# Hybrid decoder layer with a 32-expert MoE: 32 KB rows for the gate-up weights, four 4 MB places, and the add-back moved into the next gate-up

## The reference

```
out = h + merged @ w_out                       # h: (272, 1024), then only the 256 real tokens
u   = rms_norm(out)
top4 of softmax(u @ w_router)                  # 32 experts
gu  = u_rows @ w_gate_up[e] + b_gate_up[e]     # (rows, 1024) @ (1024, 2048)
gate, up = split(gu);  gate = min(gate, 7);  up = clip(up, -7, 7)
act = (up + 1) * gate * sigmoid(1.702 * gate)
y  += weight * (act @ w_down[e] + b_down[e])   # (rows, 1024) @ (1024, 1024)
```

## Time and profile before

| | us |
|---|---|
| median of 3 runs | 1257.53 |
| the runs | 1256.41 to 1257.77 |
| profiled execution, its own time | 1257.31 |
| its span (first to last instruction) | 1255.5 |
| TensorE busy in the span | 1178.8 |
| mean granted TensorE clock | 0.983 |

### The profile page before, as it was taken

The page is one execution under the profiler, slowest core; times in us unless marked ns, Lnnn a source line. Parts: engine busy times, 40 slices in busy tenths (PEclk is TensorE's granted clock), DMA queues, the critical chain, the costliest instruction groups (busy, mean ns, idle before and its releaser), DMA issues.

```text
span 1255.5 us, 14149 instructions
## 1 busy us (share of the span) xinstructions
PE 1178.8 (94%) x5825; PEld 657.1 (52%) x5825; DVE 302.8 (24%) x551; ACT 133.1 (11%) x270; POOL 4.7 (0%) x12
## 2 busy tenths in 40 slices
PE   9999999999999999999898989898898989898998
PEld 7877788888743435534352534343443434353533
DVE  2155222312302322304030303122121303030322
ACT  2233311101200000101000000001010100000000
POOL 0000001000000000000000000000000000000000
PEclk9999998999999999999999999999999999999999
DMA  9722332336799999999999999999999999999996
GB/s 380 324 98 100 110 105 97 134 116 264 278 392 423 428 428 426 430 426 426 431 428 426 429 430 428 428 429 430 426 429 430 428 428 430 429 428 429 429 420 271
DMA packets 38002, 446.37 MB, mean 356 GB/s; under 512 B 4016, under 2 KB 5168, under 8 KB 6352
## 3 DMA queue, kind: packets, MB, share of 16 engines
q1 hardware_dynamic: 37344, 443.63, 84.6%
q10 hardware_dynamic: 624, 2.25, 0.5%
HBM read 444.81 MB, written 1.05 MB: 355 GB/s over the span
## 4 chain that ended last, share of the span: by engine, by line
PE 68%; DMA 28%; issue 2%; DVE 2%; SPq 0%; ACT 0%; DVEq 0%; ACTq 0%
DMA ring<-in_w_down 23%; PE ps L511 20%; PE ps L807 18%; PE ps L830 11%; PE ps L770 5%; DMA arena<-in_w_down 4%; PE ps L796 3%; PE ps L869 3%; PE ps L851 1%; PE ps L816 1%; DVE arena L1424 1%; PE ps L825 0%; PE ps L570 0%; PE ps L643 0%; SPq L438 0%
## 5 line engine op out<-in xcount | busy, mean ns | idle before, releaser
L807 PE MATMUL ps<-ring,arena 128*64 128x512 f32 x1392 | 419.6, 614 | 36.9 <-DMA ring<-in_w_gate_up 30.5
L807 PEld LDWEIGHTS ps<-ring,arena 128*64 128x64 f32 x1392 | 137.6, 141 | 301.4 <-issue 301.4
L511 PE MATMUL ps<-arena,ring 128*128 128x256 f32 (+1 forms) x1184 | 268.2, 383 | 1.1 <-DVE arena L1305 1.1
L511 PEld LDWEIGHTS ps<-arena,ring 128*128 128x128 f32 x1184 | 221.5, 190 | 38.4 <-issue 6.6
L830 PE MATMUL ps<-ring,arena 128*64 128x512 f32 x672 | 200.9, 599 | 26.8 <-DMA arena<-in_w_down 18.0
L807 PE MATMUL ps<-arena 128*64 128x512 f32 x464 | 207.1, 599 | 0.0
L830 PEld LDWEIGHTS ps<-ring,arena 128*64 128x64 f32 x672 | 65.3, 138 | 146.3 <-issue 146.3
L1404 DVE COPY arena<-ps 128x1024 f32<-128x1024 f32 x16 | 19.6, 1224 | 420.2 <-PE ps L807 417.3
L830 PE MATMUL ps<-arena 128*64 128x512 f32 x224 | 102.0, 610 | 0.0
L1130 ACT ACTIVATE arena<-ps 128x1024 f32<-128x1024 f32 x16 | 16.4, 1023 | 583.5 <-PE ps L807 553.5
L1397 DVE TENSOR_TENSOR arena<-ps,arena 128x512 f32<-128x512 f32 x64 | 41.1, 684 | 145.8 <-PE ps L816 145.8
(11 more groups left out here) (208 smaller groups left out, 574.5 us busy)
## 6 DMA issues: line engine op xcount, KB each, us to landing
ring<-in_w_gate_up SPq DMA_DIRECT2D x95, 2048.0 KB, 26.9
ring<-in_w_down SPq DMA_DIRECT2D x47, 2048.0 KB, 24.1
arena<-in_w_gate_up SPq DMA_DIRECT2D x32, 2048.0 KB, 31.2
ring<-in_mix_w SPq DMA_DIRECT2D x37, 1024.0 KB, 5.5
arena<-in_w_down SPq DMA_DIRECT2D x16, 2048.0 KB, 26.1
ring<-in_w_down SPq DMA_DIRECT2D x2, 1024.0 KB, 30.6
arena<-in_consts ACTq DMA_DIRECT2D x1, 1424.0 KB, 12.0
arena<-in_xT SPq DMA_DIRECT2D x2, 544.0 KB, 4.3
```

The lines of the kernel that those rows point to most:

```text
L511: last = mm(ps[:, PROJ + half, 0:rhs.shape[-1]], w[:, k, half * P:(half + 1) * P], rhs, start=(k == 0), stop=(k == KC - 1))
L807: last = mm(ps[half, bank + b], columns[:, j, half], w[x][:, at:at + 512], start=(j == 0), stop=(j == 7))
```

## The change

1. **Rows and places.** From lap 3 on (`pair(2)`), gate-up weights are loaded in units of 4 MB: half of one expert, 128 rows of 32 KB, four weight rows each. There are four places of 4 MB (`quad`): three are the ring, one (`last_quad`) lies in the arena, where the order of regions and constants is changed to make it contiguous. Down units stay at 2 MB with rows of 16 KB and use halves of those places. The rows of laps 0 to 2 keep their lengths, but take other weight rows, since which weight row meets which partition now follows (h p j) with four neighbours; the copy that orders the token columns (`u2tok`) changes with it.
2. **Release.** TensorE multiplies gate-up in two halves (`gate_up_quad`), each of which waits for two 4 MB units and reports both of them used at its end. The four down units of a lap wait for the first half of the gate-up ahead of them (`gu_used`), the next gate-up for the second half and for the two halves of down (`dn_used`).
3. **Add-back.** `add_back(m - 1)` now stands between the halves of gate-up in `pair(m)`, for m from 1 on; so the bias is added in pair 1, with the add-back of lap 0. In the last pair the add-back of lap 14 still stands behind its down weights, as `add_back_by_halves`.
4. **Transition.** The expert loads start one projection unit earlier; the first unit of lap 1 is issued with unit 7 of lap 0, behind the reads of `wr`; units 6 and 7 of lap 1 wait for `gu_used` 5 and 6, where they waited for 6 and 8. The transposes of the token weights (L942 before) move from ahead of the first gate-up into it.
5. **Retention.** `rv_meta` and `rs_meta` have 128 rows, of which GpSimd sets all to zero ahead and 16 are filled, so that L634's matmuls take 128 rows. The decay constants come in a DMA of their own.

```diff
-    for name, n in (("ones", P), ("ident", P), ("heads2", P), ("halves", 2), ("eps", 1), ("eps64", 1), ("slopes", 2 * HEADS), ("fold", EXPERTS),
-                    ("tri", P), ("from_1", TOK), ("alibi", SCW), ("decay", RH * TOK), ("decay_meta", RH * TOK)):
+    for name, n in (("decay", RH * TOK), ("decay_meta", RH * TOK), ("ones", P), ("ident", P), ("heads2", P), ("halves", 2), ("eps", 1), ("eps64", 1), ("slopes", 2 * HEADS), ("fold", EXPERTS),
+                    ("tri", P), ("from_1", TOK), ("alibi", SCW)):
...
-N_CONST_EARLY = CONST_COLS["tri"][0]
+EARLY, LATE = CONST_COLS["ones"][0], CONST_COLS["tri"][0]
...
-        rv_tok, rv_meta = cut(r_rv, 0, (2, D)), cut(r_rv, 2 * D, (D,), META)
+        rv_tok, rv_meta = cut(r_rv, 0, (2, D)), cut(r_rv, 2 * D, (D,))
...
-        rs, rs_meta = cut(r_p, 0, (RH, 3 * BLK)), cut(r_p, RH * 3 * BLK, (RH, TOK), META)
+        rs, rs_meta = cut(r_p, 0, (RH, 3 * BLK)), cut(r_p, RH * 3 * BLK, (RH, TOK))
...
+        last_quad = arena[:, end_p - 2048:end_p + 6144]
+        spare = (last_quad[:, 0:4096], arena[:, end_rg - 4096:end_rg], last_quad[:, 4096:8192])
...
-        COUNT, WT, LOGIT, BIAS = 2, 3, 3, 1
+        COUNT, WT, LOGIT, BIAS = 2, 6, 3, 1
...
+        def slot_of(unit):
+            return (unit + SLOTS - 1) % SLOTS
+        homes = tuple((double(d), pair_landed[d]) for d in range(DOUBLES)) + ((spare[0], spare_landed[0]), (spare[2], spare_landed[2]))
+        def quad(m, n):
+            odd = m if isinstance(m, int) else 0
+            q = ((1 if odd % 2 else 3) + n) % 4
+            return last_quad if q == 3 else ring[:, 4 * q:4 * q + 4].rearrange("p a b -> p (a b)"), quad_landed[q]
+        def half_quad(odd, n):
+            return quad(odd, n // 2)[0][:, 4096 * (n % 2):4096 * (n % 2 + 1)]
...
-            if j == 4:
+            if j == 7:
                 return spare[1], spare_landed[1], 16
-            dst, arrived = homes[{0: 0, 1: 1, 2: 2, 3: 3, 5: 4, 7: 5}[j]]
+            dst, arrived = homes[j]
             return dst, arrived, 16
 
-        def place(m, q, odd=None):
-
-            if isinstance(m, int):
-                turn_no = 12 * m + q + 6
-                dst, arrived = homes[turn_no % 8]
-                return dst, arrived, 16 * (turn_no // 8 + 1)
-            turn_no = 12 * odd + q + 6
+        def place(m, q):
+            turn_no = 12 * m + q + 6
             dst, arrived = homes[turn_no % 8]
-            return dst, arrived, 24 * (m - odd) + 16 * (turn_no // 8 + 1)
+            return dst, arrived, 16 * (turn_no // 8 + 1)
...
+            nc.gpsimd.memset(rv_meta, 0.0).then_inc(zeros_set, 1)
+            pool.wait_ge(att_done, PAIRS)
+            nc.gpsimd.memset(rs_meta, 0.0).then_inc(zeros_set, 1)
...
-                return w_gate_up[bass.ds(2 * lap + x, 1), :, :].rearrange("o (i p j) n -> (o p) i (j n)", i=4, j=2)[:, i]
+                return w_gate_up[bass.ds(2 * lap + x, 1), :, :].rearrange("o (h p i j) n -> (o p) h i (j n)", h=2, i=2, j=2)[:, i // 2, i % 2]
...
-                i, jj = divmod(j, 2)
-                return w_gate_up[2 * lap:2 * lap + 2].rearrange("o (i p j) n -> p i j o n", i=4, j=2)[:, i, jj]
+                h, jj = divmod(j, 4)
+                return w_gate_up[2 * lap:2 * lap + 2].rearrange("o (h p j) n -> p h j o n", h=2, j=4)[:, h, jj]
+            def four_rows_source(lap, n):
+                h, x = divmod(n, 2)
+                return w_gate_up[bass.ds(2 * lap + x, 1), :, :].rearrange("o (h p j) n -> (o p) h (j n)", h=2, j=4)[:, h]
...
-                for j in (0, 1, 2, 3, 4, 5, 7):
-                    if j < 3:
-                        sp.wait_ge(proj_done, 2 * (27 + 2 * j + 1))
-                    elif j < 5:
+                for j in (0, 1, 2, 3, 7, 4, 5):
+                    if j == 7:
                         sp.wait_ge(proj_read, AT[("wr", KC - 1)] + 1)
+                        dst, arrived, _ = place(0, 0)
+                        sp.dma_start(dst.rearrange("p (o n) -> p o n", o=2), both_experts_source(1, 0)).then_inc(arrived, 16)
                     else:
-                        sp.wait_ge(proj_done, 2 * (33 + (j - 5) + 1))
+                        sp.wait_ge(proj_done, 2 * (26 + 2 * j + 1))
...
+                for q in range(1, 12):
+                    if q == 1:
 
                         sp.wait_ge(logit_folded, 1)
                         src = both_experts_source(0, 6)
                         for x, (lo, hi) in ((0, (0, 2048)), (1, (0, 1024)), (1, (1024, 2048))):
                             sp.dma_start(split_place(x, lo, hi), src[:, x, lo:hi]).then_inc(split_landed, 16)
                         sp.wait_ge(u2_turned, 2)
-                    elif q < 6:
+                    elif q < 8:
                         sp.wait_ge(gu_used, q - 1)
-                    elif q < 8:
-                        sp.wait_ge(gu_used, 2 * q - 6)
...
+            def gate_up_quads(m, odd, lap):
                 for n in range(4):
-                    dst, arrived, _ = place(m, first_q + n, odd)
-                    slot_free(m, first_q + n)
-                    src = down_both_source(lap, n // 2, n % 2)
-                    dst = dst.rearrange("p (o n) -> p o n", o=2)
-                    if n == 3 and pieces == 2:
+                    if n < 2:
+                        sp.wait_ge(gu_used, 8 * m + 6 + 2 * n)
+                    else:
+                        sp.wait_ge(dn_used, 4 * m - 6 + 2 * n)
+                    dst, arrived = quad(odd, n)
+                    sp.dma_start(dst, four_rows_source(lap, n)).then_inc(arrived, 16)
+            def down_halves(m, odd, lap):
+                for n in range(4):
+                    sp.wait_ge(gu_used, 8 * m + 10 + 2 * (n // 2))
+                    sp.dma_start(half_quad(odd, 8 + n), down_source(lap, n)).then_inc(down_landed[n], 16)
+            def last_down_units(m):
+                for n in range(4):
+                    sp.wait_ge(gu_used, 8 * m + 10 + 2 * (n // 2))
+                    dst = half_quad(0, 8 + n).rearrange("p (o n) -> p o n", o=2)
+                    sp.dma_start(dst, down_both_source(14, n // 2, n % 2)).then_inc(down_landed[n], 16)
+                for n in range(4):
+                    sp.wait_ge(gu_used, 8 * m + 14 + 2 * (n // 2))
+                    dst = half_quad(1, n).rearrange("p (o n) -> p o n", o=2)
+                    src = down_both_source(15, n // 2, n % 2)
+                    if n < 3:
+                        sp.dma_start(dst, src).then_inc(tail_landed[n], 16)
+                    else:
                         for jj in range(2):
                             part = slice(jj * D, (jj + 1) * D)
-                            sp.dma_start(dst[:, :, part], src[:, :, part]).then_inc(tail_landed[jj], 16)
-                    else:
-                        sp.dma_start(dst, src).then_inc(arrived, 16)
+                            sp.dma_start(dst[:, :, part], src[:, :, part]).then_inc(tail_landed[3 + jj], 16)
...
+                gate_up_quads(m, 0, lap_1)
+                down_halves(m, 0, lap_0)
+                gate_up_quads(m + 1, 1, lap_2)
+                down_halves(m + 1, 1, lap_1)
+            gate_up_quads(last_m, 0, 15)
+            last_down_units(last_m)
...
+            def gate_up_quad(m, odd, h):
+                w = []
+                for x in range(2):
+                    dst, arrived = quad(odd, 2 * h + x)
+                    pe.wait_ge(arrived, 16 * m - 16)
+                    w.append(dst)
+                for jj in range(4):
+                    j = 4 * h + jj
+                    for b in range(4):
+                        at = jj * 2048 + b * 512
+                        for x, half in enumerate(halves):
+                            last = mm(ps[half, GATE + b], xeT[:, j, half], w[x][:, at:at + 512], start=(j == 0), stop=(j == 7))
+                            if jj == 3 and b == 3:
+                                last.then_inc(gu_used, 2)
...
+            def add_back_by_halves(m):
+                for b in range(4):
+                    pe.wait_ge(eout_ready, 2 * m + 1 + b // 2)
+                    pe.wait_ge(added, 4 * m - 1 + b)
+                    for c in range(2):
+                        at = (2 * b + c) * P
+                        last = mm(add_ps[:, b % 2, c], e_out[:, at:at + P], selwT, start=True, stop=True)
+                    last.then_inc(summed, 1)
...
+                pe.wait_ge(wgt_ready, 1)
+                for t in range(2):
+                    last = turn(ps[0:EXPERTS, WT, t * P:(t + 1) * P], wgt[:, t], ident)
+                last.then_inc(wgt_turned, 1)
...
-                        gate_up(i, lambda q: place(m, q, odd), xeT)
+                    for h in range(2):
+                        if h == 1:
+                            pe.wait_ge(selwT_ready, m)
+                            pe.wait_ge(eout_ready, 2 * m)
+                            add_back(m - 1, isinstance(m, int) and m == 1)
+                        if odd is None:
+                            for i in (2 * h, 2 * h + 1):
```

(24 more changed lines are left out.)

99 lines of the change are left out of this document (38 added, 61 removed).

## The result

| | before | changed |
|---|---|---|
| median of the runs, us | 1257.65 (4 runs, 1256.41 to 1259.43) | 1269.2 (4 runs, 1267.59 to 1271.39) |
| ratio, with its 95% interval | | 1.0095 (1.0080 to 1.0111), slower |
| span of the profiled execution, us | 1255.5 | 1266.4 |
| TensorE busy, us | 1178.8 | 1183.1 |

The changed kernel is 0.95% slower, 11.6 us, and the interval is clear of no change. Forecast were 1254.7 us and a range of 1250.0 to 1259.7; the time lies outside it, on the side of rival C.

The account below looks back on a forecast made before the run. TensorE was taken to bound the first part and the end, the full DMA queue the expert part. −3.4 − 4.8 − 0.3 + 5.7 = −2.8 from 1257.31 gave 1254.5, as a median 1254.7 us; range 1250.0 to 1259.7.

Parts of the forecast that it names:

- rival C: Expert loop: release too late in each of 13 pairs, queue runs dry; 1263.8 us, slower than before; chance 0.10.
- Places of 4 MB and release in halves: Expert loop: the added wait of down units for the first half of gate-up costs 0.
- the slack of 2.7 us: Expert loop, first half's report: 19.4 us of loads less 1.2 to first packets and 15.5 to report leaves 2.7 us.
- Rows of 32 KB: Gate-up loads of laps 3 to 15: merging 16 KB rows saves 11.5 ns per engine each, −4.8 us.
- The end: After the last gate-up landing: TensorE has half a gate-up left instead of a quarter, +5.7 us.
- Transition: Start of expert loads: hole at 371 us mostly filled, 0.8, against 0.5 lost in pair 2; −0.3 us.
- Retention: Retention, 196.5 to 203.2 us: 128 rows instead of 16 keep TensorE's clock from falling to half, −3.4 us.
- Rival A: Retention: the clock falls anyway, so the part brings 0 instead of −3.4; 1258.1 us; chance 0.10.

Follow-up runs that it names:

- a2: Changed kernel with the add-back one quarter earlier, inside the first half of gate-up, so the first report comes later: 1298.69 us, ratio 1.0332.
- q1: Changed kernel with gate-up reported by quarters and down units laid so a lap's first two need only the first quarter: 1261.06 us, ratio 1.0034.
- a5: Changed kernel, release in halves kept, but 4 MB places filled by 2 MB loads and TensorE starting on each landed quarter: 1253.62 us, ratio 0.9968.
- b2: Kernel before with only the release in halves: from pair 2 on down units wait for half of the next gate-up: 1258.23 us, ratio 1.0014.
- q5: q4 with rows of 16 KB, each 4 MB place filled by two loads: 1259.23 us, ratio 1.0024.
- q4: q1 with pair 2's first four 4 MB loads waiting for the same counts as in the changed kernel: 1256.75 us, ratio 0.9994.
- q6: q4 with lap 15's gate-up in eight 2 MB loads and TensorE waiting for them by quarters: 1251.07 us, ratio 0.9949.
- q7: q4 with 16 rows again in retention's meta matmuls, zeroing kept: 1257.42 us, ratio 1.0002.
- b1: Kernel before with the retention part alone, zeroed operands of 128 rows and two fills: 1254.73 us, ratio 0.9978.

## Why the prediction was wrong

Five terms, in the prediction's order, and what became of each.

*Places of 4 MB and release in halves, 0 in the loop.* **This is the step that failed.** The mechanism was set out rightly (SP stands at the wait for the first half, 19.4 us of cover, a start only at the landing), and rival C named it; the slack of 2.7 us was mis-sized, in two terms. The landing gap of the two halves was 19.4 as forecast.

The first term is the report. From the landing to SP's issue it took 16.4 us in the mean (15.7 to 17.2) and not 15.5. The half itself took 15.4 to 16.9 us, six times of eleven over 16, so half clock cost 2.2 in the mean behind this wait of 4.6 to 6.7 us and not the 1.7 taken from the earlier trace rows, and the steps from landing to start and from end to issue, 0.14 and 0.17, had been left out.

The second term is the cover. 19.4 us run to the landing of the last unit, and the prediction counts them as if all 16 engines had work until then. They have not. In this stage of the changed kernel no row starts, though the unit ahead, issued at 766.1, lands only at 795.4:

```profile
792.70:793.60 0.90, 0.90 (x5) 0.80 (x5) 0.00 (x0) 0.00 (x0) 0.00 (x0) 1.00 0.00 0
```

By the packets the last 16 rows of gate-up end on average 1.8 us ahead of the landing, in single pairs 0.9 to 2.7, and 0.5 of that lie between the last row and the landing. With about 1.2 us from the issue to an engine's first row, the prediction's figure and a2's mean, it is 19.4 − 1.8 − 1.2 − 16.4 = 0.0 instead of 2.7. Rival C had its point at 18.2 us, which was 1.8 too high: by these numbers, an estimate, it is 16.4.

At a slack of nothing the single pair decides. At 834 and 776 us the reports came 16.5 and 16.7 us behind the landing, nearly alike, but the engines ended 0.9 and 2.5 us ahead of theirs, and they idled 0.0 and 1.2 us. Over the eleven pairs the mean idle is about 0.6 us and the first 16 rows behind the issue take 1.04 us instead of 0.61: 1.0 us together, where the pairs are 0.9 us longer than in q1, 59.3 against 58.4, 0.9 × 11 = 10 us in all. That also says why the landing gaps are not in step with the reports: idle time ahead of the last landing is not in them.

q1 and a5 take the loss away from either side, by a finer report or an earlier start; b2 shows that the coarse report alone is harmless in the loop where TensorE starts early. What put the price at zero was half clock taken from rows with a shorter wait, and a cover counted to a landing. Why the engines of one load end up to 2.7 us ahead of its landing stays open.

*Rows of 32 KB, −4.8 us.* Right in kind, a little high in size. 32 KB rows came at 8.39 MB / 19.42 us = 432 GB/s (432.6 forecast) and a pair at 58.4 us instead of 58.7 or 58.8 (q1, q5): 0.3 to 0.4 × 13 = 4 to 5 us, measured 2.5 to 3.8 between q5 and q4, where the second report takes part of it back. The changed kernel has this gain too, and lost more than twice as much in the holes.

*The end, +5.7 us.* Right: 52.4 us against 46.7, and q6 takes back 5.7.

*Transition, −0.3 us.* It came out as a loss. The hole at 371 us is filled (share 1.11), but the loss in pair 2 was 1.8 and not 0.5: the stage at 492 us has a share of 0.68. b2, which has that wait too, paid its 1 to 2 us there. Of the filled hole no gain is left to see: the lead at the start of the expert part was 2.8 us, less than the 3.6 of the first gather below. (The 1.8 is from comparing, in both traces, the time by which the queue had moved the same bytes, ahead of this place and behind it.)

*Retention, −3.4 us.* The stage shows 1.00 and L663 took 3.45 us, as forecast, and the first gather started 3.6 us sooner. But the price was that of one execution. With 16 rows the clock fell fully in the trace before, for a shorter time in q7 and not at all in b2; with 128 rows it fell there in none of ten traces. The mean gain is what b1 shows, 2.2 us, or the 0.7 to 1 of q7, and that the rows are the cause is shown only as a tendency. Rival A, by which the part brings nothing, has b1 against it. In the changed kernel's trace the gain was also partly given back: the gather behind it, 3.81 us before, met a low clock and took 5.44. It did so in five of the thirteen traces, all with 128 rows in retention, where five others with 128 rows show 3.81.

```profile
333.51 5.44 PE L799 MATMUL ps<-arena 128*128 128x128 f32 x32 [0.95 <-DVE arena L1434]
```

The sum: −2.8 at the start of the expert part and +1.8 in pair 2, both by the same comparison, +10 of holes in the loop, −3.6 for the rows (two halves come 19.42 us apart with long rows and 19.56 with short ones, so 13 × 0.28; the comparison itself can't tell the rows from the holes), +5.6 at the end: +11.0, and the spans differ by 10.9.

## What to carry to other kernels

Where a queue is the bound and buffers are few, the time that decides runs from the landing of a piece to the report that it is used, and it contains the work on the whole piece, at the clock that follows a wait, and the start of the next transfer. The cover against it ends before the landing of what is still queued, here 1.8 us in the mean. Starting and reporting on larger pieces lengthened the time here; a larger transfer can still be kept if the consumer reports in finer steps (q1, q4), or a coarse report if it starts on finer ones (a5). Size such a slack by rows from the case that will be, with the longer wait in it, and call it zero when it comes out under the scatter of single laps.

## What was not expected of the hardware

- A DMA issued into an empty queue (a2) landed 7.5 to 7.8 us later, where its 2.1 MB take 4.9 us in a running queue. Its first row started 1.0 us behind the issue, and the first 16 rows of 16 KB took 1.30 us each instead of 0.61.
- The 16 DMA engines don't end a load together: in the changed kernel their last rows ended 0.9 to 2.7 us, on average 1.8, ahead of the landing of the load.
- Behind a wait of 4.6 to 6.7 us half a gate-up took 15.4 to 16.9 us, at full clock 13.93. Filling 3.9 us of that wait moved the time at half clock to the next wait.
- The same instructions may or may not meet the half clock: in retention with 16 rows the stage from 196.5 to 203.2 us showed 0.50 in the kernel before, 1.00 in b2, which is the same code up to there, and 0.75 in q7.
